# Score levels of a decayed scan with half of the query columns

## The reference, cut to what matters

```python
def step(S, inp):
    qc, kc, lfc, vc = inp
    b = jnp.cumsum(lfc, axis=2)
    inter = jnp.einsum('bhtd,bhde->bhte', qc * jnp.exp(b), S)
    diff = b[:, :, :, None, :] - b[:, :, None, :, :]
    decay = jnp.exp(jnp.where(mask, diff, -jnp.inf))
    A = jnp.einsum('bhtsd,bhsd->bhts', qc[:, :, :, None, :] * decay, kc)
    intra = jnp.einsum('bhts,bhse->bhte', A, vc)
    ...
    return S_new, inter + intra
```

## Time and profile before

| | |
|---|---|
| median of 3 runs | 3482.2 us (3480.15 to 3487.68) |
| the profiled execution | 3480.85 us, its span 3479.0 us |
| PE busy | 3008.3 us, 86% of the span |
| PEld (weight loads) busy | 2710.1 us |
| DVE busy | 1648.7 us, 47% |
| ACT busy | 698.5 us, 20% |
| POOL busy | 933.9 us, 27% |
| mean granted TensorE clock | 0.927 |

### The profile page before, as it was taken

The page is one execution under the profiler, slowest core; times in us unless marked ns, Lnnn a source line. Parts: engine busy times, 40 slices in busy tenths (PEclk is TensorE's granted clock), DMA queues, the critical chain, the costliest instruction groups (busy, mean ns, idle before and its releaser), DMA issues.

```text
span 3479.0 us, 45020 instructions
## 1 busy us (share of the span) xinstructions
PE 3008.3 (86%) x18988; PEld 2710.1 (78%) x18988; DVE 1648.7 (47%) x2077; ACT 698.5 (20%) x1134; POOL 933.9 (27%) x508
## 2 busy tenths in 40 slices
PE   6999788876769857999899994798999999989887
PEld 6889677766757856777777773577999999978887
DVE  3689366663131125444444444531245665555445
ACT  3010112212132222000000001331122222233331
POOL 7332231112111112223232231132323223212343
PEclk9997899898979987999999997799999999999999
DMA  5122221101220021111111113233233423245662
GB/s 189 56 92 72 90 65 41 43 31 37 87 101 25 25 97 68 43 36 52 44 38 47 36 48 115 97 121 109 82 107 104 122 92 98 98 158 188 219 243 89
DMA packets 138959, 304.74 MB, mean 88 GB/s; under 512 B 10136, under 2 KB 76592, under 8 KB 138672
## 3 DMA queue, kind: packets, MB, share of 16 engines
q10 hardware_dynamic: 102512, 170.32, 14.3%
q1 hardware_dynamic: 36288, 132.14, 11.7%
HBM read 224.81 MB, written 77.61 MB: 87 GB/s over the span
## 4 chain that ended last, share of the span: by engine, by line
PE 71%; DVE 13%; issue 6%; ACT 3%; DMA 2%; POOL 2%; ACTq 2%; DVEq 0%
PE pp L201 28%; PE pp L216 23%; PE pp L1610 6%; PE pp L1954 3%; POOL w_lo L2515 1%; PE pp L1126 1%; PE pp L1135 1%; PE pp L1137 1%; PE pp L1514 1%; DVE ffn_cb L536 1%; PE pp L1494 1%; DVE gdn_C L1312 1%; PE pp L418 1%; PE pp L1158 1%; DMA close_m<-ma_s 1%
## 5 line engine op out<-in xcount | busy, mean ns | idle before, releaser
L2513 POOL CAST w_hi<-w_raw 128x1024 fp32r<-128x1024 f32 x252 | 292.0, 1159 | 2498.8 <-PE pp L201 1055.2
L216 PE MATMUL pp<-w_hi,act_hi 128*128 128x256 f32 (+1 forms) x2752 | 801.2, 291 | 53.6 <-ACT hg_st L1823 22.7
L216 PE MATMUL pp<-w_lo,act_hi 128*128 128x256 f32 (+1 forms) x2752 | 789.3, 287 | 0.0
L216 PE MATMUL pp<-w_hi,act_lo 128*128 128x256 f32 (+1 forms) x2752 | 789.3, 287 | 0.0
L2515 POOL TENSOR_TENSOR w_lo<-w_raw,w_hi 128x1024 fp32r<-128x1024 f32 x252 | 648.6, 2574 | 20.2
L216 PEld LDWEIGHTS pp<-w_hi,act_hi 128*128 128x128 f32 x2752 | 543.6, 198 | 61.3 <-ACT hg_st L1823 22.9
L216 PEld LDWEIGHTS pp<-w_lo,act_hi 128*128 128x128 f32 x2752 | 543.2, 197 | 0.0
L216 PEld LDWEIGHTS pp<-w_hi,act_lo 128*128 128x128 f32 x2752 | 542.4, 197 | 0.0
L201 PE MATMUL pp<-act_hi,w_hi 128*128 128x512 f32 x1408 | 437.9, 392 | 31.5 <-ACTq L90 18.7
L201 PE MATMUL pp<-act_lo,w_hi 128*128 128x512 f32 x1408 | 436.2, 391 | 0.0
L201 PE MATMUL pp<-act_hi,w_lo 128*128 128x512 f32 x1408 | 436.0, 391 | 0.0
(11 more groups left out here) (373 smaller groups left out, 3946.0 us busy)
## 6 DMA issues: line engine op xcount, KB each, us to landing
w_raw<-in_weights SPq DMA_DIRECT2D x252, 512.0 KB, 3.6
z_s<-hg_st ACTq DMA_DIRECT2D x24, 1024.0 KB, 4.6
hg_qkb<-hT_s ACTq DMA_DIRECT2D x24, 512.0 KB, 6.2
qkvT_s<-mixin_o ACTq DMA_DIRECT2D x12, 512.0 KB, 2.8
gdn_qkv<-qkvT_s ACTq DMA_DIRECT2D x8, 768.0 KB, 5.6
front_x<-in_x ACTq DMA_DIRECT2D x8, 512.0 KB, 7.1
norm_mix_x<-in_x ACTq DMA_DIRECT2D x8, 512.0 KB, 3.6
x_s<-mix_y ACTq DMA_DIRECT2D x8, 512.0 KB, 2.6
```

Of the source, the lines that this page charges most:

```text
L216: last = pe.matmul(dst, a[:, k, t * P:(t + 1) * P], w[slot][:, k * SC:k * SC + n], start=(k == 0 and a is high and w is w_hi), stop=(k == ...
L2513: pool.tensor_copy(hi, raw).then_inc(w_split, 1)
```

## The change

Levels 0 to 6 multiply only the upper columns of each block, 64 per head, and their result is compact: 64 columns per head, 512 in all, in one PSUM bank. The selective copy writes the upper columns of `A` from it, with the mask's upper columns. Level 0 drops the lower differences and lower factors: its exponential takes only the upper columns, and the stationary operand of its product is the keys as loaded. TensorE's wait for `cp` of two levels back stands ahead of that for `kup`. The diagonal is as before.

```diff
 def level(t, l):
     after(act, V, f"eup{l}", t)
-    A.done(act.activation(self.E[l % 2][:, :, :], self.E[l % 2][:, :, :], ACT.Exp), f"x{l}")
+    e = self.E[l % 2][:, :, :] if l else self.upper(self.E[0], 0)
+    A.done(act.activation(e, e, ACT.Exp), f"x{l}")
...
     U.make_to(pe, m[l])
+    if l >= 2:
+        after(pe, V, f"cp{l - 2}", t)
     if l < LEVELS:
         after(pe, V, f"kup{l}", t)
-        lhs = rhs = self.KQ[l % 2]
-    else:
-        lhs, rhs = self.qkb[s][:, 1], self.qkb[s][:, 0]
-    if l >= 2:
-        after(pe, V, f"cp{l - 2}", t)
     for h in range(HH):
-        last = pe.matmul(pp[l % 2][:, h * P:(h + 1) * P], lhs[:, h, :], rhs[:, h, :], start=True, stop=True)
+        if l < LEVELS:
+            lhs = self.KQ[l % 2] if l else self.qkb[s][:, 1]
+            last = pe.matmul(self.scores(l)[:, h], lhs[:, h, :], self.upper(self.KQ[l % 2], l)[:, h], start=True, stop=True)
+        else:
+            last = pe.matmul(pp[l % 2][:, h * P:(h + 1) * P], self.qkb[s][:, 1, h, :], self.qkb[s][:, 0, h, :], start=True, stop=True)
...
-    V.done(tt(ev[:, :, 0, :], mid, bv[:, :, 0, :], ALU.subtract), f"elo{l}")
-    V.done(tt(ev[:, :, 1, :], bv[:, :, 1, :], mid, ALU.subtract), f"eup{l}")
+    if l:
+        V.done(tt(ev[:, :, 0, :], mid, bv[:, :, 0, :], ALU.subtract), f"elo{l}")
+    V.done(tt(ev[:, :, 1, :], bv[:, :, 1, :], mid, ALU.subtract), *((f"eup{l}",) if l else ("elo0", "eup0")))
...
-    V.done(tt(kv[:, :, 0, :], halves(k, sz)[:, :, 0, :], ev[:, :, 0, :], ALU.mult), f"klo{l}")
-    V.done(tt(kv[:, :, 1, :], halves(q, sz)[:, :, 1, :], ev[:, :, 1, :], ALU.mult), f"kup{l}")
+    if l:
+        V.done(tt(kv[:, :, 0, :], halves(k, sz)[:, :, 0, :], ev[:, :, 0, :], ALU.mult), f"klo{l}")
+    V.done(tt(kv[:, :, 1, :], halves(q, sz)[:, :, 1, :], ev[:, :, 1, :], ALU.mult), *((f"kup{l}",) if l else ("klo0", "kup0")))
...
+def upper(self, x, l):
+    return x[:, :, :].rearrange("p h (b two n) -> p h b two n", two=2, n=1 << l)[:, :, :, 1, :]
+
+def scores(self, l):
+    return pp[l % 2][:, 0:HH * P // 2].rearrange("p (h b n) -> p h b n", h=HH, n=1 << l)
+
 def pick(self, dve, t, l):
     after(dve, self.pes, f"a{l}", t)
     after(dve, self.dves, f"cp{l - 1}" if l else "zero", t)
     self.dves.done(dve.memset(self.mark[:, :], 0.0), f"at{l}")
-    self.dves.done(dve.copy_predicated(
-        self.A[:, :, :], up_masks[:, l, :].rearrange("p (a n) -> p a n", a=1).broadcast_to((P, HH, P)),
-        pp[l % 2][:, :].rearrange("p (h n) -> p h n", h=HH)), f"cp{l}")
+    if l < LEVELS:
+        sz = 1 << l
+        picked = up_masks[:, l, :].rearrange("p (a b two n) -> p a b two n", a=1, two=2, n=sz)[:, :, :, 1, :]
+        self.dves.done(dve.copy_predicated(
+            self.upper(self.A, l), picked.broadcast_to((P, HH, P // (2 * sz), sz)), self.scores(l)), f"cp{l}")
+    else:
+        self.dves.done(dve.copy_predicated(
+            self.A[:, :, :], up_masks[:, l, :].rearrange("p (a n) -> p a n", a=1).broadcast_to((P, HH, P)),
+            pp[l % 2][:, :].rearrange("p (h n) -> p h n", h=HH)), f"cp{l}")
```

## The result

The changed kernel is slower. Its median is 3499.46 us (12 runs, 3490.94 to 3507.57); the kernel before, timed in the same rounds, has 3484.04 us (12 runs, 3479.93 to 3489.54). The ratio is 1.0044, with the interval 1.0033 to 1.0055. I had said 3481.0 in a range of 3472 to 3489 and given "slower" a chance of 0.07: the forecast was wrong. The profiled execution of the changed kernel took 3496.17 us (span 3494.4), against 3480.85 (3479.0) of before.

The account below looks back on a forecast made before the run. TensorE was taken to bound the scan stage (66.90 busy of 67 us a later tile). Products 0, copies 0 (hidden), wait 0, one stall -0.6 summed to -0.6 us: 3481.0 us forecast, range 3472 to 3489.

Parts of the forecast that it names:

- slower: Whole kernel over 0.2% slower, by a dearer selective copy, a falling TensorE clock or strided moving columns; chance 0.07 together.
- What of this reaches the path: Scan stage: lighter VectorE and ScalarE work stays hidden behind TensorE; only one first-tile stall shrinks, -0.6 us.
- Products, 0 us saved: Score products, levels 0 to 6: weight load paces each record, so 64 moving columns save 0 us; other bound 49.9.
- Rival B: Score products: 64-column records come faster as part of the load hides; fully, 3431 us; chance 0.08.
- Copies: 56 selective copies on VectorE: 0.83 us each instead of 1.36, 30 us of VectorE's time, hidden from the path.
- rival C: Selective copy: strides and short runs make it dearer, VectorE bounds a level; at 2.72 us a copy, 3493; chance 0.03.
- Level 0: Level 0: one subtraction and multiplication fewer per tile, 10.5 us of VectorE; ScalarE's exponential at most 0.53 us shorter.
- The moved wait, 0 us: TensorE's wait for the copy two levels back, now before the query factor's: last wait is the same, 0 us.
- Stalls of before: TensorE's scan-stage waits: the first tile's 0.65 us stall comes about 0.6 sooner; the 1.3 us at the transposes stays.
- Rival D, the clock: Scan stage: TensorE's clock falls for want of columns; one level per tile at half clock gives 3519 us; chance 0.02.
- Rival E: Score products: strided fp32 moving columns cost TensorE more; at four times, level 0 alone gives 3496 us; chance 0.02.

Follow-up runs that it names:

- e2: The changed kernel timed once more, nothing altered: 3502.29 us, ratio 1.0042 to the kernel before.
- e1: Kernel before with level 0 alone in the new form (64-column products, short copy, no lower half): 3498.53 us, ratio 1.0026.
- e4: Kernel before with only the selective copies of levels 0 to 6 changed, reading the upper 512 columns at a stride: 3500.78 us, ratio 1.0031.
- e7: Changed kernel with level 0 wholly as before, levels 1 to 6 new: 3487.37 us, ratio 0.9994.
- e6: Changed kernel with GpSimd's weight split started five projection units later in each later tile: 3486.75 us, ratio 1.0001.
- e13: Kernel before with GpSimd's weight split started five projection units later in each later tile: 3486.93 us, ratio 1.0000.
- e5: Changed kernel with VectorE making a level's factors before the next level's differences: 3498.14 us, ratio 1.0038.
- e11: Changed kernel with GpSimd's split five units later and only each block's lower columns as stationary operand at levels 5 and 6: 3476.07 us, ratio 0.9965.
- e14: Kernel before with a 256-element VectorE fill between the level-0 copy and level 3's differences: 3499.27 us, ratio 1.0035.
- e15: Kernel before with a 64-element VectorE fill between the level-0 copy and the next operation: 3498.80 us.
- e17: Changed kernel with a 128-element VectorE fill between the level-0 copy and the next operation: 3503.47 us.
- e12: Changed kernel with a 256-element VectorE fill between the level-0 copy and level 3's differences: 3509.06 us, ratio 1.0052.
- e16: Changed kernel with a 64-element VectorE fill between the level-0 copy and the next operation: 3498.31 us.

## Why the prediction was wrong

**The step that failed** is "What of this reaches the path": "About 40 us less work for VectorE and 4 for ScalarE are hidden by TensorE's 66.90 busy us of 67. The closest cover is at level 3 ... this cover grows." I looked for work that becomes longer on the path and found none, and took less work to be at worst free. That step put the effect of VectorE's lighter work at nothing, and the runs showed a stall of TensorE of 1.47 us in each of seven tiles in its place. I treated VectorE's durations as its own. They are not: in the earlier trace rows stands a 512-element difference that took 1.52 us, where the earlier trace rows has 0.63 and 0.68 for such operations, and I used it as a start and a sum without asking what had held it up. GpSimd's own timeline, with its 4.74 us subtraction and 2.70 for the next one of the same form, I did not read. The earlier trace rows had GpSimd busy 18.23 us a later tile. So I counted the path's cover for the level after the meeting (0.73 us at level 3), and missed that the meeting itself could turn round one level sooner. There the trace of before held the numbers for it: level 2's query factor ended at 2714.99 + 0.68 = 2715.67, 5.73 us after the first product of level 0 at 2709.94, and was wanted at 2 x 4.66 = 9.32, a cover of 3.6 us. Stretched by 2.18, 0.84 and 2.18, as the changed kernel's three operations were, it comes 5.2 us later: 1.6 late. Two of these sizes, 0.84 and 2.18, stood in the next level of the trace of before (1.52 and 2.86 for 0.68). Measured are 1.47 of stall and 1.63 of distance.

**The size.** Stalls, 7 x 1.70 = 11.9 us, and one clock fall of 1.5 in the profiled execution: 13.4, less the small gain at the first tile. The medians' 15.4 us is of the same size; what of it is more than 13.4 no run shows for certain, but e2's profile has two falls. Which edit brings the stalls is shown by e1, e4 and e7 (level 0's), which meeting by e6 and e13 (GpSimd's split); and e5 shows that the lateness, once there, comes out in another place if its first outlet is closed.

**Point by point.**

- *Products, 0 us saved:* right. A block of 16 records takes 1.73 us with 64 columns, where it was 1.78, and the unit behind it 2.93 where it was 2.88: 4.66 us a level, unchanged. Rival B did not happen. e11 shows from the other side that the stationary columns are what counts.
- *Copies:* 0.70 us at level 2, rising to 0.76 at level 6 (0.83 forecast, bound 0.68), but 1.34 and 1.29 at levels 0 and 1, where the runs are one and two elements long. So the term was mis-sized: the 56 copies took 76.3 us and now take 50.1, 26.2 us less instead of 30. This is the first half of rival C, dearer short runs; but 1.34 is far under the 2.35 from which a copy would decide by its length, and the mechanism of C is not what happened.
- *Level 0:* its exponential takes 0.66 us instead of 1.06; VectorE's work of a later tile is 39.76 us and not some 37, since the stretched operations count as busy, 5.2 us of them here against 3.0 before.
- *The moved wait, 0 us:* right; no wait for a copy stands at a product except through the late query factor behind it.
- *Stalls of before:* the 0.65 us at the first tile went, as forecast, and the 1.3 us at the transposes stayed.
- *Rival D, the clock:* right in part, and small. As I put it, a want of columns alone was to do it, and the 64-column products of e6 and e7 brought no fall. The clock fell in the stalling kernels. None in before, e6, e7 and e13, which have no stalls ahead of level 2; 1 to 4 in the stalling kernels with 64-column products; none in e1, e4, e14 and e15, which stall just as long but keep 128 moving columns from level 1 on. So in this table stalls and the 64-column products were both there whenever it fell. They were not enough: six of the changed kernel's seven stalls passed without a fall. It makes the difference between 1.0044 or 1.0042 for the changed kernel and 1.0026 and 1.0031 for e1 and e4, at about 1.5 us a fall (one of e17's and two of e12's lasted twice as long and cost 3.1); the intervals overlap in part, so the traces' counts carry this more than the ratios.
- *Rival E:* no sign of it. Level 0's strided block is 1.89 us by the timeline, and so are those of the next level.
- *Not among my rivals:* a lighter VectorE that loses its turn. My "slower" cases were about an operation that gets dearer or a clock that falls.

Here two sentences of the Trainium skill bear on what was seen. Its page "SBUF — State Buffer", sections "🔬 SBUF: two separate sides" and "Who interferes with whom", says that VectorE and GpSimd share a pair of ports that one instruction holds to its end, and that a VectorE operation with two SBUF inputs meets a GpSimd operation that reads SBUF there, while one with at most one SBUF input (outside its two-port modes) doesn't. The traces agree, both GpSimd operations here reading SBUF: only two-input operations are stretched (2.86 and 1.52 for 0.68 us), while a selective copy, which reads the scores from PSUM, keeps its time beside them (1.37 us at 2716.59, beside the last part of GpSimd's 4.74 us). Had I weighed this rule against the earlier trace rows, it would have named this rival. The page also says "Whoever issues first gets the shared pair". On this the traces are not with it as far as recorded starts go: in e14 GpSimd starts 0.27 us ahead and waits, and why it waits for one operation in most kernels and for four in two, or for either in one kernel's second meeting, the sentence doesn't tell. The measurement decides.

## What to carry to other kernels

Before work is taken off an engine that is not the bound, look for its operations of one shape that differ in duration: they can mark where it meets another engine, as here. There an edit that moves VectorE's first operation by about 0.05 us (e16 and e17 against before, each with a fill ahead of it) can go with the other order, and once the order differed between tiles without any such shift. Ask what the reverse would cost (here 5.2 us against 3.6 of cover, in each of seven tiles), and if the meeting can be moved to where there is slack, move it first (e6). And of a product with fp32 operands, cut the stationary columns rather than the moving ones while the load of weights sets the pace.

## What the runs showed of the hardware

- Two engines' order at a meeting was one of two, with nothing between. At level 0 it was the same in all seven later tiles of an execution: all stalled, or none did. At the next level of the kernel before it was not: GpSimd's cast took 3.35 us in two tiles and 1.53 to 1.55 in five. GpSimd's subtraction of 1024 elements took 2.38 us alone, 2.77 to 3.12 with one VectorE operation let through, and 4.74 with four.
- A selective copy of 512 elements costs 1.34 us in runs of one element, 1.29 in runs of two (1.32 in e6) and 0.70 to 0.76 in runs of 4 to 64; 1024 contiguous ones cost 1.36.
- 16 fp32 records take 1.73 us with 64 moving columns and 1.78 with 128 at 128 stationary columns, but 1.07 with 64 stationary ones; 32 records with 32 take 0.63, or 0.020 us each, where their columns alternate between two parts of the array.
- A clock fall came after TensorE had been idle 1.47 us and then run 16 records of 64 columns in 1.97, once in seven such places of the changed kernel. About the same idle time with 128-column records (1.43 to 1.72 us) left the clock at 1.00 in e1, e4, e14 and e15.
